# Seven block products for eight over half of the k tiles, in pairs of column tiles, with every loop written out

## The chip, the cores and the metric

The kernel runs on 1 core of one Trainium2 chip. The metric is the device time of one launch in microseconds: the median of the runs, 3132.33 us before (three runs, 3132.25 to 3133.17). TensorE multiplies, VectorE (DVE) and ScalarE (ACT) work on tiles, GpSimd (POOL) and SyncE (SP) here mostly issue DMAs.

## The reference

One layer of a hybrid decoder for a prompt of 512 rows and 8 single sampled rows with caches, all fp32. Cut to what matters:

```python
u = rms_norm(h, g_pre)                                   # (rows, 2048)
z = jnp.einsum('bsd,de->bse', u, w_in)                   # 176 column tiles of 128 are used
qa, ka, va, za, qr, kr, vr, zr, ga, gb = jnp.split(z, split_points, axis=-1)
# attention: 3 groups (window, dilation) x 8 heads, mixed by their softmax denominators
ya = combine_groups(outs, lses).reshape(B, S, A_WIDTH) * jax.nn.silu(za)
# retention: 8 heads, keys and values of 256, decay per head, root mean square norm per head
yr = (yr * rsqrt(mean(yr * yr) + EPS) * g_ret) * jax.nn.silu(zr)
merged = sigmoid(ga) * (ya @ w_a_out) + sigmoid(gb) * (yr @ w_r_out)
h = h + rms_norm(merged @ w_o, g_post)
h = h + sigmoid(h @ w_ple_gate) * (p @ w_ple_proj)
```

The outputs are also the new windows of keys and values (for the sampled rows a copy of the caches moved by one row) and the new retention states.

## The kernel before

All activations stand transposed: `U` ("moving") holds 16 k tiles of 128 features by 520 columns (512 prompt rows and 8 sampled ones, `TC` = 520, `HC` = 260). Precision comes from two parts: every operand is split into a rounded part (hi) and the rest (lo), and a product is three passes, hi x hi, hi x lo, lo x hi.

The work is cut into units. A unit is one column tile of a weight matrix (128 columns): `unit` (L462) runs 16 k tiles x 3 passes x 2 halves of 260 columns = 96 matmuls into two PSUM banks of `acc`, which has two such accumulators used in turn. There are 176 units over `u` (10 for each of 8 attention heads, 8 for each of 8 retention heads, 4 in each of 8 rounds of gates), then 16 each for `w_a` (8 k tiles), `w_r`, `w_o` and `w_gate`. The mean times of the trace carry the line of the matmul, L475.

The weights of a unit come by one DMA of 1 MB on SyncE's queue (`load`, L402) into one of two slots of `raw`, and behind it a piece of the cache copies from DRAM to DRAM (`keep_rows`, L365). ScalarE rounds all 2048 elements in one instruction (`hi`, L818, L821), VectorE subtracts (`lo`, L1136, L1139) and raises `s_wready`; TensorE waits for that and for `s_accfree`. ScalarE also takes a finished unit out of PSUM (`head_tile` L893, `residue_tile` L899, gates L1028).

Between k tiles of a unit hang hooks: the small matmuls and transposes of the head's own work, at places written out by hand (`attention_head` L612, `retention_head` L721). Each waits for its inputs: `exchange` (L568) for `spread_stats` on VectorE, `prob_turn` (L578) for the probabilities, `head_rows` and `ret_rows` for a finished tile, `ret_scores` and `ret_values` for PSUM banks and decayed scores, `sample_states` (L711) for the new states of half of the sampled rows, `sample_values` for weighted value rows. VectorE does in program order, unit by unit: row copies, `masked_far`, `masked_near`, `maxima`, `spread_stats`, `shares`, `normed`, `sample_keys` (L1307), `sample_columns` (L1405), `sample_states` (L1425), `scaled_keys`, `decayed`, and `ret_output` (reciprocal, scaling, gate; L1517 to L1525), with `lo` after the rest of the unit.

The heads after the first (for retention after the second), the gate rounds after the second and the projections run as hardware loops on every engine, with wait values worked out in registers (`Tally`, `Waits`).

## Time and profile before

| | before |
|---|---|
| median of the runs | 3132.33 us |
| the profiled execution | 3126.95 us |
| its span, first to last instruction | 3125.4 us |
| TensorE busy | 3026.9 us, 97% |
| VectorE busy | 1128.4 us, 36% |
| ScalarE busy | 827.4 us, 26% |
| mean granted TensorE clock | 0.987 |
| matmuls of 260 columns in L475 | 22,080 |

The busy time of TensorE is that of a pipelined stream, so the cost of one matmul is read from the start and end of a long run of them, and not from the mean duration of one. "Issue" as the reason of an idle stretch is time in which the engine waited for nothing that the profile shows. Idle time of an engine off the path costs nothing. The stages are: to 60 us the transposes, the norm and the projection of `p`; to some 1120 us the attention heads; to some 2040 us the retention heads; to 2410 us the gates; then the four projections.

### The profile page before, as it was taken

What the parts mean: (1) busy time and instruction counts of PE and PEld (TensorE: products, weight loads), DVE (VectorE), ACT (ScalarE), POOL (GpSimd) and SP (SyncE); (2) the same over time, 40 slices, a digit from 0 to 9 for tenths busy, and PEclk for the clock granted to TensorE, in tenths of its full rate; (3) what the DMA queues carried; (4) which work ended last, traced back from release to release, by engine and by line L of the source; (5) the groups of instructions that cost most, each with busy time, mean ns of one, the idle gap of its engine ahead of it and who ended that gap; (6) DMA issues with size and microseconds to landing.
All of it is one profiled execution on the core that took longest, in us unless ns stands there. A gap on an engine that the chain in (4) does not pass through costs nothing.

```text
span 3125.4 us, 58547 instructions
## 1 busy us (share of the span) xinstructions
PE 3026.9 (97%) x24438; PEld 2975.1 (95%) x24438; DVE 1128.4 (36%) x1325; ACT 827.4 (26%) x1065; POOL 369.7 (12%) x553
## 2 busy tenths in 40 slices
PE   7999999999999999999999999999999999999798
PEld 7999999999999998999999999999999999999798
DVE  5324233242323323453443443352222343322632
ACT  6223232222322222222222222222122221222222
POOL 2000000000000000220221121121000100100410
PEclk9999999999999999999999999999999999999899
DMA  9665646565565644654654554577655576755352
GB/s 312 201 202 188 209 155 210 187 200 195 167 217 182 198 136 127 192 163 126 189 177 125 181 169 139 179 238 248 212 193 171 170 253 201 248 166 169 108 179 77
DMA packets 534990, 574.97 MB, mean 184 GB/s; under 512 B 15560, under 2 KB 495624, under 8 KB 531592
## 3 DMA queue, kind: packets, MB, share of 16 engines
q1 hardware_dynamic: 490944, 428.31, 43.2%
q0 software_dynamic: 43856, 143.69, 14.0%
q8 instruction: 173, 2.83, 0.4%
q14 instruction: 17, 0.14, 0.0%
HBM read 515.67 MB, written 232.42 MB: 239 GB/s over the span
## 4 chain that ended last, share of the span: by engine, by line
PE 94%; DVE 2%; issue 1%; ACT 1%; DMA 1%; DVEq 0%; ACTq 0%; SPq 0%; POOL 0%; POOLq 0%
PE acc L475 84%; PE aux L648 1%; PE aux L658 1%; PE aux L667 1%; PE aux L717 1%; DVE stage_buffers L1670 1%; PE aux L547 1%; PE aux L603 0%; PE aux L554 0%; PE aux L641 0%; PE aux L675 0%; PE aux L708 0%; PE acc L538 0%; PE aux L574 0%; PE aux L588 0%
## 5 line engine op out<-in xcount | busy, mean ns | idle before, releaser
L475 PE MATMUL acc<-moving,weights 128*128 128x260 f32 x22080 | 2748.1, 285 | 45.2 <-issue 32.7
L475 PEld LDWEIGHTS acc<-moving,weights 128*128 128x128 f32 x22080 | 2687.6, 189 | 61.7 <-issue 49.3
L1139 DVE TENSOR_TENSOR weights<-raw_weights,weights 128x2048 fp32r<-128x2048 f32 (+1 forms) x242 | 538.8, 2226 | 1299.4 <-ACT weights L821 1284.0
L821 ACT ACTIVATE weights<-raw_weights 128x2048 fp32r<-128x2048 f32 (+1 forms) x242 | 451.3, 1865 | 213.4 <-PE acc L475 204.4
L896 ACT ACTIVATE stage_buffers<-acc 128x520 f32<-128x520 f32 x96 | 58.1, 605 | 854.6 <-PE acc L475 854.4
L902 ACT ACTIVATE stage_buffers<-acc 128x260 f32<-128x260 f32 x48 | 30.9, 643 | 394.8 <-PE acc L475 394.8
L1707 POOL DMA_DIRECT2D out<-stage_buffers x72 | 50.0, 694 | 670.1 <-DVEq L1222 507.0
L1028 ACT ACTIVATE stage_buffers<-acc 128x520 f32<-128x520 f32 x32 | 19.4, 606 | 264.6 <-PE acc L475 257.0
L1788 POOL DMA_DIRECT2D out<-stage_buffers x64 | 45.5, 715 | 135.0 <-DVEq L1447 123.5
L1740 POOL DMA_DIRECT2D stage_buffers<-in_cache_win x24 | 21.7, 905 | 333.4 <-DVE sample_keep L1312 230.0
L1431 DVE SCALAR_TENSOR_TENSOR stage_buffers<-stage_buffers,sampled 128x256 f32<-128x256 f32 x128 | 52.1, 479 | 13.7 <-ACT stage_buffers L975 13.6
L1707 POOL DMA_DIRECT2D sg_scr<-stage_buffers x32 | 17.4, 543 | 306.3 <-ACTq L1029 281.0
L1684 DVE TENSOR_TENSOR stage_buffers<-stage_buffers 128x520 f32<-128x520 f32 x16 | 11.2, 701 | 116.6 <-ACTq L1116 116.6
L1879 POOL TENSOR_TENSOR stage_buffers<-stage_buffers 128x520 f32<-128x520 f32 x16 | 27.0, 1696 | 218.7 <-DVE stage_buffers L1670 218.7
L1630 DVE TENSOR_TENSOR stage_buffers<-acc,stage_buffers 128x520 f32<-128x520 f32 x16 | 11.2, 698 | 112.1 <-PE acc L475 112.1
L1655 DVE TENSOR_TENSOR stage_buffers<-stage_buffers 128x520 f32<-128x520 f32 x16 | 11.2, 701 | 110.6 <-ACTq L1093 110.6
L489 PE MATMUL acc<-moving,weights 128*128 128x260 f32 x192 | 28.5, 306 | 18.3 <-DVE moving L1674 18.3
L1777 POOL DMA_DIRECT2D stage_buffers<-in_state_ret x64 | 45.3, 713 | 6.9 <-issue 4.3
L489 PEld LDWEIGHTS acc<-moving,weights 128*128 128x128 f32 x192 | 26.1, 207 | 20.9 <-issue 13.0
L1707 POOL DMA_DIRECT2D vrow_scr<-stage_buffers x8 | 4.1, 513 | 348.7 <-DVEq L1507 348.7
L1781 POOL DMA_DIRECT2D stage_buffers<-vrow_scr x64 | 45.0, 709 | 0.0
L1707 POOL DMA_DIRECT2D y_scr<-stage_buffers x24 | 13.2, 549 | 267.3 <-DVE stage_buffers L1525 125.6
(230 smaller groups left out, 1626.0 us busy)
## 6 DMA issues: line engine op xcount, KB each, us to landing
raw_weights<-in_w_in SPq DMA_DIRECT2D x176, 1024.0 KB, 5.8
out<-in_cache_win SPq DMA_DIRECT2D x128, 1023.5 KB, 8.5
out<-in_cache_win SPq DMA_DIRECT2D x32, 1022.0 KB, 7.9
out<-stage_buffers POOLq DMA_DIRECT2D x120, 256.0 KB, 3.3
stage_buffers<-in_cache_win POOLq DMA_DIRECT2D x48, 512.0 KB, 7.1
stage_buffers<-in_state_ret POOLq DMA_DIRECT2D x64, 256.0 KB, 5.6
raw_weights<-in_w_r_out SPq DMA_DIRECT2D x16, 1024.0 KB, 6.0
raw_weights<-in_w_o SPq DMA_DIRECT2D x16, 1024.0 KB, 5.8
```

The costliest lines, as they stand in the source:

```text
L475: mm = pe.matmul(acc[:, par, half, 0:HC], W[:, par, wp, k, :], U[:, up, k, a:b], start=(k == ks[0] and n == 0), stop=(k == ks[-1] and n == 2))
L489: mm = pe.matmul(acc[:, par, half, 0:HC], W[:, par, wp, k, :], U[:, up, k, a:b], start=(k == 0 and n == 0), stop=(k == KD - 1 and n == 2))
L547: mm = pe.transpose(aux[:, bank, tb * P:(tb + 1) * P], src[:, tb * P:(tb + 1) * P], ident[:])
L648: mm = pe.matmul(aux[:, bank, 0:T - jb * P], rk[:, j, jb * P:(jb + 1) * P], rq[:, j, jb * P:T], start=(j == 0), stop=(j == 1))
L821: act.activation(W[:, par, 0, 0:k], raw[:, par, 0:k], ACT.Copy).then_inc(s_whi, 1)
L896: act.activation(halves(dst), acc[:, par, :, 0:HC], func, scale=scale).then_inc(ready, 1)
L1139: dve.tensor_tensor(W[:, par, 1, 0:k], raw[:, par, 0:k], W[:, par, 0, 0:k].bitcast(F32), ALU.subtract).then_inc(s_wready, 1)
L1431: dve.scalar_tensor_tensor(out=r_st[:, half, b, j, :], in0=r_v[:, half, b, :], scalar=zs[:, bass.ds(h * 2 * NS + at, 1)], in1=r_st[:, half ...
L1707: pool.dma_start(dst, src).then_inc(stored, 16)
L1777: pool.dma_start(r_st[:, half, b], state[0, half * HB + b, bass.ds(h, 1)].rearrange("o (j p) e -> p (o j) e", p=P)).then_inc(s_rst[half], 16)
L1781: pool.dma_start(r_v[:, half, b].rearrange("p (e c) -> p e c", e=2), v_src[b:b + 1].broadcast_to([P, 2, P])).then_inc(s_rst[half], 16)
L1788: pool.dma_start(ret_s[0, half * HB + b, bass.ds(h, 1)].rearrange("o (j p) e -> p (o j) e", p=P), r_st[:, half, b]).then_inc(s_rnewst[half ...
```

## The change

**The product.** Of the 88 pairs of units over `u`, 86 are computed by Strassen's scheme in Winograd's form over the last eight k tiles. The two column tiles of a pair, the two groups of 4 k tiles (8 to 11, 12 to 15) and the two halves of the columns make 2 x 2 x 2 blocks. Seven block products of 4 k tiles x 3 passes = 12 matmuls stand in for eight. Four combinations of the moving blocks are made once, in the first pairs (`combine_blocks`, into `V` and into `U[:, :, 8:12, HC:TC]`). Four sums of weight blocks are made for every pair on VectorE, inside `lo`. The first eight k tiles stay as they were. The products add up partly in PSUM and partly by way of `part`: ScalarE copies three half banks of a pair out (`s_read`), VectorE one (`s_read7`), and VectorE makes the final tiles with additions (`evict`).

**The order.** A pair is 11 operations (steps) of 12 or 24 matmuls. `W` becomes a ring of 6 chunks of 4 k tiles (`AHEAD`): `hi` and `lo` work on 512 elements for the operation six ahead. `raw` holds one pair in two halves of eight k tiles (before: two slots), each loaded when its last reader of the pair before is done. The heads' small work hangs on the 11 steps on all engines. Row copies go from VectorE to ScalarE; taking out finished u tiles goes from ScalarE to VectorE; SiLU and sigmoid become their own operations on ScalarE.

**The rest.** All loops are written out, and wait values are constants. Sampled states go two rows at a time (`QB`), not four; the third group of value rows is loaded into the second's buffer. `pp_out` has 8 tiles, not 16. `X` has 8 tiles and the residual sum is made in `M`. The projections are plain pairs in chunks of 4 k tiles. The number of cache copies is the same; in attention and gates two are issued behind each pair's loads.

```diff
+OPS = {"S": [("sum", 0), ("raw", 3, 0), ("raw", 0, 0), ("raw", 1, 0), ("raw", 2, 0), ("raw", 2, 1), ("raw", 3, 0),
+             ("sum", 0), ("raw", 3, 1), ("raw", 0, 1), ("raw", 1, 1)],
...
+AHEAD = 6
...
-    W = stack.enter_context(nc.sbuf_tensor("weights", [P, 2, 2, KD, P], F32R))
-    raw = stack.enter_context(nc.sbuf_tensor("raw_weights", [P, 2, KD, P], F32))
+    W = stack.enter_context(nc.sbuf_tensor("weights", [P, AHEAD, 2, 4, P], F32R))
+    raw = stack.enter_context(nc.sbuf_tensor("raw_weights", [P, 2, 8, 2, P], F32))
...
+        def load(p, half):
+
+            sp.wait_ge(s_wready, read_until[p.nth, half] + 1)
...
+        for p in pairs:
+            for half in halves_of(p):
+                load(p, half)
+            q = p.nth
+            if q < RET:
+                for j in range(2):
+                    keep_rows(sp, 2, q // 5, 2 * (q % 5) + j)
...
+        def strassen_pair(p, hooks):
+            g = p.first
+            for n in range(p.n):
+                for f in hooks.get(n, ()):
                     f()
+                pe.wait_ge(s_wready, g + n + 1)
+                if n == 0:
+                    acc_ready(0)
+                    mm = product(g + n, 0, 1, moving(8, 1), True, True)
+                elif n == 1:
+                    mm = product(g + n, 0, 0, moving(12, 0), True, False)
+                elif n in (2, 3):
+                    product(g + n, 0, 0, moving(4 * (n - 2), 0), False, n == 3)
+                    if n == 2:
+                        pe.wait_ge(s_read, 3 * p.sums + 1)
+                    mm = product(g + n, 0, 1, moving(4 * (n - 2), 1), False, False)
+                elif n == 4:
+                    acc_ready(1)
+                    mm = product(g + n, 1, 1, moving(8, 0), True, True)
+                elif n == 5:
+                    mm = product(g + n, 1, 0, combined(1), True, True)
+                elif n == 6:
+                    mm = product(g + n, 0, 1, moving(12, 1), False, True)
+                elif n == 7:
+                    pe.wait_ge(s_read, 3 * p.sums + 2)
+                    mm = product(g + n, 1, 1, combined(0), False, True)
+                elif n == 8:
+                    pe.wait_ge(s_read7, p.sums + 1)
+                    mm = product(g + n, 1, 0, combined(2), False, False)
+                else:
+                    product(g + n, 1, 0, moving(4 * (n - 9), 0), False, n == 10)
+                    if n == 9:
+                        pe.wait_ge(s_read, 3 * p.sums + 3)
+                    mm = product(g + n, 1, 1, moving(4 * (n - 9), 1), False, n == 10)
+                mm.then_inc(s_used, 1)
...
+        for h in range(H):
+            hooks = [
+                {2: [row_turn], 4: [values]} if h else {},
+                {},
+                {2: [lambda: head_rows(kT[:, 0, :], 2)], 4: [lambda: head_rows(kT[:, 1, :], 0)],
+                 5: [lambda: scores_far(1)], 6: [lambda: scores_near(0)], 8: [lambda: scores_near(1)]},
+                {2: [lambda: head_rows(kT[:, 2, :], 1)], 3: [lambda: scores_far(2)], 10: [exchange]},
+                {2: [lambda: head_rows(vT[:, 0, :], 0)], 4: [lambda: head_rows(vT[:, 1, :], 0)],
+                 6: [lambda: prob_turn(0)], 7: [lambda: prob_turn(1)], 8: [lambda: prob_turn(2)],
+                 9: [lambda: prob_turn(3)], 10: [lambda: head_rows(vT[:, 0, :], 0)]},
+            ]
...
+        STATE_AT = {(0, 8): [lambda: sample_states(0)], (1, 2): [lambda: sample_states(1)],
+                    (1, 7): [lambda: sample_states(0)], (2, 1): [lambda: sample_states(1)]}
...
+                {2: [lambda: ret_rows(rk, 0, 2, 0)], 3: [lambda: ret_rows(rk, 1, 0, 1)], 5: [lambda: ret_scores(0)],
+                 6: [lambda: ret_scores(1)], 8: [lambda: ret_scores(2)], 9: [lambda: ret_scores(3)]},
+                {1: [sample_values] if h >= 2 else [], 2: [lambda: ret_rows(rv, 0, 0, 0)],
+                 3: [lambda: ret_rows(rv, 1, 0, 1)], 5: [vrow_turn], 6: [lambda: ret_values(0)],
+                 7: [lambda: ret_values(1)], 8: [ret_state], 10: [ret_norm]},
...
+        def lo(g):
...
+            if strassen and n == 0:
+                dve.wait_ge(s_wload[1], 16 * loads_due[p.nth, 1])
+                dve.drain()
+                dve.tensor_tensor(tmp_w[:], raw_chunk(2, 1), raw_chunk(3, 1), ALU.add).then_inc(s_sum, 1)
...
+            if strassen and n == 1:
+                dve.drain()
+                dve.tensor_tensor(raw_chunk(2, 1), raw_chunk(2, 0), raw_chunk(2, 1), ALU.subtract)
+                dve.tensor_tensor(tmp_w[:], tmp_w[:], raw_chunk(2, 0), ALU.subtract)
+                dve.drain()
+                dve.tensor_tensor(raw_chunk(3, 0), raw_chunk(3, 0), tmp_w[:], ALU.subtract).then_inc(s_sum, 1)
...
+        def steps(p, tiles, hooks, scale=1.0):
+
+            g = p.first
+            for n in range(p.n):
+                if p.mode == "S":
+                    if n == 5:
+                        dve.wait_ge(s_read, 3 * p.sums + 2)
+                        evict(p, 0, 0, tiles[0], scale)
+                        dve.wait_ge(s_used, g + 6)
+                        dve.scalar_tensor_tensor(out=part[:, 0, :], in0=acc[:, 1, 0, 0:HC], scalar=scale, in1=part[:, 0, :],
+                                                 op0=ALU.mult, op1=ALU.add).then_inc(s_read7, 1)
+                    if n == 7:
+                        dve.wait_ge(s_read, 3 * p.sums + 3)
+                        evict(p, 0, 1, tiles[0], scale)
+                    if n == 10:
+                        dve.wait_ge(s_used, g + 11)
+                        for half in range(2):
+                            evict(p, 1, half, tiles[1], scale)
...
+                for f in hooks.get(n, ()):
+                    f()
+                lo(g + n + AHEAD)
...
+                { 4: [lambda: masked_far(2, h), lambda: maxima(1)],
+                 8: [lambda: sample_keys(2, h - 1)] if h else [], 9: [spread_stats]},
+                {0: [gaps], 2: [shares, normed],},
...
+            return {(0, 4): [lambda: sample_states(0, h)], (0, 9): [lambda: sample_states(1, h), lambda: sample_ret_y(0, h)],
+                    (1, 3): [lambda: sample_ret_y(1, h), lambda: sample_states(2, h)],
+                    (1, 8): [lambda: sample_states(3, h), lambda: sample_ret_y(2, h)],
+                    (2, 2): [lambda: sample_ret_y(3, h)]}
...
+            return {(1, 5): [lambda: sample_columns(i)], (2, 10): [lambda: last_sample_columns(i)],
+                    (3, 3): [lambda: sample_output(i)]}
```

In the tables of hooks a key (j, n) is pair j of a head and step n; on TensorE a hook runs before operation n, on VectorE after the evictions of step n and before its `lo`. `ret_output` hangs on (0, 1), `scaled_keys` on (2, 4), `decayed` on (2, 6), (2, 7), (2, 9) and (2, 10).

## Rows read from the trace of the kernel before

**Rows 1.** The page, busy time, share of the span and instructions.
```profile
PE 3026.9 (97%) x24438; PEld 2975.1 (95%) x24438; DVE 1128.4 (36%) x1325; ACT 827.4 (26%) x1065; POOL 369.7 (12%) x553
```

**Rows 2.** Windows by stage: busy (instructions) by engine, PEclk, DMA share, GB/s.
```profile
100.00:1250.00 1150.00, 1124.08 (x9150) 1113.42 (x9149) 379.27 (x429) 304.94 (x501) 81.88 (x123) 0.99 0.57 184
1250.00:2100.00 850.00, 840.12 (x6581) 806.62 (x6581) 367.21 (x525) 214.47 (x237) 165.14 (x247) 1.00 0.55 169
```

**Rows 3.** Groups by line: busy us, mean ns of one | idle before.
```profile
L1139 DVE TENSOR_TENSOR weights<-raw_weights,weights 128x2048 fp32r<-128x2048 f32 (+1 forms) x242 | 538.8, 2226 | 1299.4 <-ACT weights L821 1284.0 <-DMA stage_buffers<-in_c_move 14.9
...
L875 ACT ACTIVATE moving<-stage_buffers 128x520 fp32r<-128x520 f32 x16 | 10.2, 636 | 5.5 <-PE acc L538 2.2 <-DVE stage_buffers L1201 1.8 <-issue 0.4
```

**Rows 4.** The waits: who waited for whom, us in total, times, longest.
```profile
DVE weights L1139 <- ACT weights L821: 1284.0, 221, 12.7
```

**Rows 5.** Timeline of TensorE: start, us, instructions in a row.
```profile
999.74 46.37 PE L475 MATMUL acc<-moving,weights 128*128 128x260 f32 x384
```

**Rows 6.** Timeline of the weight loads in `values`, one PSUM bank.
```profile
1119.41 1.87 PEld L603 LDWEIGHTS aux<-stage_buffers 128*128 128x128 f32 x16
```

**Rows 7.** Timeline at a turn of the attention loop, then two of the retention loop.
```profile
317.97 0.86 PE L475 MATMUL acc<-moving,weights 128*128 128x260 f32 x5 [1.50 <-issue]
320.77 6.92 PE L475 MATMUL acc<-moving,weights 128*128 128x260 f32 x43 [1.94 <-issue]
...
1463.05 28.88 PEld L475 LDWEIGHTS acc<-moving,weights 128*128 128x128 f32 x240 [1.99 <-issue]
...
1577.88 22.26 PEld L475 LDWEIGHTS acc<-moving,weights 128*128 128x128 f32 x185 [1.77 <-issue]
```

**Rows 8.** Windows behind a turn, and behind an idle of 2.7 us.
```profile
322.00:326.00 4.00, 4.00 (x23) 4.00 (x23) 0.00 (x0) 0.00 (x0) 0.56 (x1) 0.58 0.80 235
326.00:330.00 4.00, 4.00 (x36) 4.00 (x35) 0.29 (x1) 0.00 (x0) 0.00 (x0) 1.00 0.88 353
...
1243.00:1247.00 4.00, 4.00 (x23) 4.00 (x23) 0.00 (x0) 0.00 (x0) 1.22 (x3) 0.57 0.19 70
```

**Rows 9.** Timeline of VectorE in the norm, operations back to back.
```profile
45.05 0.75 DVE L1201 SCALAR_TENSOR_TENSOR stage_buffers<-stage_buffers,small 128x520 f32<-128x520 f32 x1
45.72 0.69 DVE L1208 TENSOR_TENSOR moving<-stage_buffers,moving 128x520 fp32r<-128x520 f32 x1
46.33 0.75 DVE L1201 SCALAR_TENSOR_TENSOR stage_buffers<-stage_buffers,small 128x520 f32<-128x520 f32 x1
```

**Rows 10.** Groups by line: the operations of VectorE's hooks.
```profile
L1310 DVE TENSOR_TENSOR stage_buffers<-stage_buffers 128x1024 f32<-128x1024 f32 x24 | 29.2, 1218 | 0.0
...
L1485 DVE TENSOR_SCALAR stage_buffers<-aux,small 128x128 f32<-128x128 f32 x64 | 18.0, 344 | 4.7 <-PE aux L641 2.2 <-issue 2.2
...
L1228 DVE SCALAR_TENSOR_TENSOR stage_buffers<-stage_buffers,small,aux 128x512 f32<-128x512 f32 x16 | 11.2, 744 | 2.5 <-issue 2.4
...
L1248 DVE TENSOR_REDUCE stage_buffers<-stage_buffers 128x4 f32<-128x1024 f32 x8 | 9.8, 1220 | 0.8
```

**Rows 11.** Timeline of VectorE in a retention head: `ret_output`, `sample_states`.
```profile
1466.01 3.34 DVE L1517 RECIPROCAL stage_buffers<-stage_buffers 128x512 f32<-128x512 f32 x1
...
1471.13 1.29 DVE L1525 TENSOR_TENSOR stage_buffers<-stage_buffers 128x512 f32<-128x512 f32 x2
...
1493.84 3.26 DVE L1431 SCALAR_TENSOR_TENSOR stage_buffers<-stage_buffers,sampled 128x256 f32<-128x256 f32 x8 [2.64 <-ACT stage_buffers L975]
...
1498.58 1.67 DVE L1444 SCALAR_TENSOR_TENSOR stage_buffers<-stage_buffers,sampled 128x256 f32<-128x256 f32 x4 [0.17 <-issue]
```

**Rows 12.** DMA issues: size, median us from issue to landing.
```profile
raw_weights<-in_w_in SPq DMA_DIRECT2D x176, 1024.0 KB, 5.8
out<-in_cache_win SPq DMA_DIRECT2D x128, 1023.5 KB, 8.5
...
pp_scr<-stage_buffers POOLq DMA_DIRECT2D x4, 1040.0 KB, 10.8
```

**Rows 13.** Timeline of the weight loads before the second gate projection unit.
```profile
2939.01 4.46 PEld L475 LDWEIGHTS acc<-moving,weights 128*128 128x128 f32 x24 [4.56 <-DVE weights L1139]
```

1826 lines of the change are left out of this document (949 added, 877 removed).

## The prediction

> **What bounds the kernel now.** I read the page's engine shares first: TensorE is busy 97% of the span, 3026.9 of 3125.4 us [rows 1]. The stage table then says that this holds in the attention stage (100 to 1250 us) and in the retention stage (1250 to 2100 us), with VectorE busy 33% and 43% there [rows 2]. The costly groups show why VectorE is busy at all: half of it is L1139 (`lo`), one subtraction of 2048 elements per unit, 2.23 us each [rows 3], after the copy of L821 (`hi`) on ScalarE. The waits show that it has slack: VectorE waited 1284 us for `hi`, which itself waits for a whole unit of 96 matmuls [rows 4]. So TensorE's stream sets the end. In it 384 matmuls of 260 columns run in 46.37 us, 0.1203 us each once the last one's own latency is off [rows 5]. That is the price of a matmul.
>
> **Matmuls removed.** Of the 88 pairs of u units, 86 take the new scheme (the first two stay plain). Such a pair had 192 matmuls; now it has 96 over the first eight k tiles and 7 x 12 over the last eight, 180. 86 x 12 x 0.1203 = -124.1 us. Twelve in a row now write one PSUM bank where before two banks alternated. The nearest row is the 16 matmul halves of L603, which accumulate in one bank at 0.112 us for 128 columns of plain fp32 [rows 6]; that is two passes of the columns and no more, so I take no price for it. Bounds: 0 and 0.012 us on each of the 7224, +87.
>
> **Loops removed.** At each turn of the attention loop TensorE stood idle 1.50 and 1.94 us for "issue" [rows 7], and for 4 us behind it the granted clock was near its lower level, 1.2 GHz: 23 matmuls in 4 us and not 36 [rows 8]. That is 5.0 us a turn, seven turns, -35. The retention loop shows one gap of 1.99 or 1.77 us between weight loads at each of five turns [rows 7], some 1.6 of it lost, -8; the clock stays. At the seams between stages, of which the wait of 4.56 us for weights at 2939 is one [rows 13], the finer weight chunks make the next weights ready early. I count 17 us of such idle that goes and 6 that comes (the last tile before the gate projection is followed by more matmuls, and the last two output turns stand at the end): -11.
>
> **The start.** `pp_out` shrinks to 8 tiles, so ScalarE waits from the ninth for a store that takes 10.8 us to land [rows 12]: +8. In the first plain pair VectorE now stops at op 2 for the last such store and combines the moving blocks (8 operations of 1040 elements, about 1.15 us each, twice the rate of [rows 9]), and three more at op 6, before it evicts at op 7. TensorE is done with that pair 23.1 us after its start and needs the accumulator; by my count VectorE gives it 9 us later. +10 (0 to +15).
>
> **What each pair now costs VectorE.** Operations of 520 elements start 0.61 to 0.67 us apart, waits included, and end 0.69 us after their start [rows 9]. A pair has 11 `lo` of 512 (6.9 us), four weight sums with drains (3.0 us), and the evictions that ScalarE did (5 operations of 252 or 260 elements, two small, drains: 2.8 us): 12.7 us where two `lo` took 4.5. TensorE needs 21.65 us for a pair. [...]
>
> The average therefore fits; the order is what hurts. Each engine runs its list in order, and TensorE now waits for VectorE inside the pair: at op 8 for `s_read7` (VectorE's step 5), at op 9 and at op 2 for partial sums, at op 0 for the accumulator, and at every hook. Count from the end of op k, e_k: without hooks e0 1.4, e2 5.8, e4 10.1, e7 14.4, e8 15.9, e9 18.8, e10 21.7 us (12 matmuls 1.44 us, 24 matmuls 2.89). Weights for op k+6 are ready 1.5 us after e_k (a copy of 520 on ScalarE takes 0.64 [rows 3], the subtraction 0.69, and handovers). The next pair's half buffer can be asked for after `lo` of op 8, at e2+1.5, and a load of 1 MB lands 5.8 us later [rows 12]: 13.5 us. From there VectorE does sum, `lo`, `lo`, three sums, eviction, three `lo` and reaches step 10 at 21.7, just as TensorE does; part 0 is copied by 23.6 and wanted at 26.0. A pair without hooks costs no stall, with 2.4 us to spare.
>
> **Attention, fourth pair of a head.** e3 is 9.9 with its hooks. VectorE after it: `lo` 11.4; `masked_far`, `maxima` (0.74 and 1.22 [rows 10], drains) 13.7; `lo` 14.3; eviction and seventh product 15.2; sum, the trip to ScalarE and back 17.3; `lo` 17.9; sums 20.2; eviction 21.0; `lo` 21.6; `sample_keys` (two of 1.22 us [rows 10]) 24.1; `lo` 24.7; `spread_stats` 25.2. `exchange` stands before op 10 and waits for it, and TensorE is there at 20.1: 5.1 us. In the fifth pair `shares` and `normed` delay the load by 1.5 us, and `head_rows` of v and a bank cost 1.3; the second pair 0.2. An idle of 2.7 us before 1243 us was followed by 23 matmuls in 4 us [rows 8], 1.5 us lost, so I add 1.7. Seven heads x 8.3 and 4 in the first: +62. What this part gives in matmuls and loops is inside the terms above.
>
> **Retention, a head from the third on.** First pair: ScalarE's `ret_gate` is done at 4.7, `lo` at 6.0; then `ret_output`, 6.3 us of reciprocal, scaling and gating [rows 11], to 12.2; three `lo` 14.0; `sample_states` for two samples, half of the 6.4 us that [rows 11] show for four plus its drains, 3.6 us, to 17.6; `lo`, eviction, seventh product: 19.1. TensorE is at op 8 at 14.4 and has 0.95 us of its own hook there: 3.75 us. With `sample_states` again at step 9, twice in the second pair, and 3.9 us of `sample_columns` (three operations of 1024 elements [rows 10]) VectorE has 57 us of chain in two pairs where TensorE has 46: stalls of 0.8 (part 0), 1.4 (part 2 at op 9, ScalarE held by the late sum), 1.65 (`sample_states` hook of the third pair). In the third pair `scaled_keys` (8 of 0.344 [rows 10]) holds the scores 1.3 and `decayed` 1.4; the last columns at step 10 hold `sample_values` 3.0, the v rows 0.3. Together 13.6 us; six heads 82, second head 11, first 2. The clock behind the stalls of 3 us: +10 to +14, I take 14. Sum +109.
>
> **Gates.** The last head's work falls into pairs 0 to 7 without TensorE's hooks to cover it: 3.75+0.8+1.4+1.65+2.5+2.5, clock 2: +14.
>
> **The sum.** 3125.4-124.1-35-8-11+8+10+62+109+14 = 3150 us of span. The profiled run took 3126.95 us for its span of 3125.4, and the median of the runs is 3132.33, so the median lies 6.9 us over the span: 3157 us. No part of the sum is larger than the stalls, 185 us of it. Under 0.2% (6.3 us) a measurement of this kernel can't tell a change from none.
>
> **Rivals.** (a) *The stalls swallow one another.* A wait at op 8 gives VectorE and the load time that the next one then doesn't need; I followed that through in the retention head, but only within it. Against it: `exchange` and op 8 stand behind pure VectorE work. For it: the average, 12.7 of 21.65 us before hooks. If 40% of the 185 remain: 3157-111 = 3046, with 55% 3074, with 30% 3027. (b) *No stall at all*, the change as written: 3157-185-10 = 2962. The waits speak for slack [rows 4], the in-order lists against it. (c) *The load is late, the slower side.* One pair's raw weights now sit in a single buffer and two cache copies of 8.5 us each [rows 12] are queued at once behind the load of half 0. If half 1 lands after 8.2 us and more, the 2.4 us of slack are gone, and each of the 86 pairs pays what lies over it; with the queue's 8.5 us and the hooks that already use the slack, about 0.7 us a pair: +60, 3217. It decides from a landing of 8.2 us. (d) *The matmuls don't get cheaper*, because one bank at a time costs 0.012 us each: +87, 3244.
>
> **Chances.** The sum as worked out 0.50, from 3110 to 3200 by itself (0.10 of it under 3126, 0.08 within 0.2%); (a) 0.28, nearly all faster; (b) 0.05; (c) 0.14; (d) 0.03. Faster 0.05+0.27+0.10 = 0.42, same 0.08, slower 0.50. The range leaves out (b) and the high ends of (c) and (d): 3027 to 3225 us.
>
> **What the changed profile would show.** Right: 21,048 matmuls of 260 columns; no "issue" gaps of 2 us; VectorE near 57% (1128 us before, plus 8.2 us for each of 86 pairs, less 33 us of row copies that go to ScalarE); TensorE idle of 5 us before `exchange` in each head from the second on, and of 3 to 4 us before op 8 in each retention head's first pair; a retention head of some 123 us where a turn of the loop took 114.8 (1463.05 to 1577.88 [rows 7]); gates faster than before. Wrong: if idle of TensorE in the two stages stays under 60 us, (a) or (b) holds; if VectorE's first sum waits for the load in most pairs, (c); if a run of 12 matmuls takes over 1.5 us, (d). The weakest step is the order inside the retention head, then the 0.62 us for each small operation, which enters it some fifteen times a pair.

## The result, and the profile after

The changed kernel takes 3308.03 us (median of four runs, 3301.25 to 3311.07) against 3132.48 of the kernel before in the same session: a ratio of 1.0557, 95% interval 1.0539 to 1.0575. Slower was forecast, by 0.8%; it is 5.6%, and 3308 lies outside the range of 3027 to 3225. The profiled run has a span of 3308.8 us.

The page of the changed kernel, engine shares and granted clock, to be read beside [rows 1]:

```profile
PE 3017.6 (91%) x23406; PEld 2950.6 (89%) x23406; DVE 1760.2 (53%) x3159; ACT 1122.3 (34%) x2078; POOL 361.8 (11%) x537
...
PEclk8999999999999899899999999999999999999799
```

TensorE has 1032 matmuls less and is busy for only 9 us less. That is the first hint: matmuls worth 124 us are gone, and 115 us came back inside the busy time. The stages tell where. Their limits are found by counting matmuls of 260 columns (in both kernels: start of the u units, start of retention, of the gates, of the projections). Columns: length, busy time and instructions of TensorE, of its weight loads, VectorE, ScalarE, GpSimd; granted clock, DMA share, GB/s. First before, then after:

```profile
60.20:1122.10 1061.90, 1038.60 (x8512) 1033.18 (x8513) 347.97 (x394) 287.88 (x479) 72.25 (x108) 0.99 0.60 194
1122.10:2036.80 914.70, 903.86 (x7034) 865.45 (x7033) 372.78 (x516) 225.59 (x258) 158.13 (x236) 1.00 0.52 159
2036.80:2415.60 378.80, 377.08 (x3143) 376.80 (x3142) 106.95 (x102) 89.39 (x73) 40.77 (x68) 1.00 0.66 217
2415.60:3125.40 709.80, 665.82 (x5463) 660.31 (x5462) 264.69 (x253) 182.82 (x196) 82.36 (x112) 0.98 0.54 173
```

```profile
71.20:1182.10 1110.90, 1022.36 (x8034) 1013.56 (x8035) 625.64 (x1138) 397.99 (x808) 72.20 (x108) 0.94 0.55 183
1182.10:2210.80 1028.70, 919.22 (x6674) 870.94 (x6673) 596.99 (x1142) 330.86 (x574) 159.78 (x238) 0.94 0.42 141
2210.80:2589.60 378.80, 363.85 (x2950) 361.97 (x2950) 221.12 (x396) 150.03 (x274) 29.51 (x43) 0.97 0.61 219
2589.60:3308.80 719.20, 668.23 (x5462) 662.85 (x5460) 279.15 (x408) 200.19 (x347) 84.08 (x120) 0.97 0.51 175
```

Idle is length less busy. The column "clock" is what is left of the change in busy time once the removed matmuls (0.1203 us each) are taken off. In us against before, measured, and what the prediction had put there:

| | matmuls | idle | clock | sum | predicted idle, clock, sum |
|---|---|---|---|---|---|
| start | | | | +11 | +8 |
| attention (first pair in it) | -55 | +65 | +39 | +49 | +36, +1, -18 |
| retention | -46 | +99 | +62 | +114 | +87, +14, +55 |
| gates | -23 | +13 | +10 | 0 | +12, +2, -9 |
| projections, seams | | | | +9 | -11 |
| all | -124 | +177 | +110 | +183 | +25 |

That the column is time at the lower clock can be read directly: busy time times what the granted clock lacks to 1, added up over windows of 1 us, is 135 us in the changed kernel and 26 in the one before, 109 more (attention 43, retention 51, gates 10; some 4 us of the 62 are hooks of the last attention head that now stand behind the border). So the idle was 42 us above the prediction's 135, and the clock 93 above its 17.

Timeline of TensorE in an attention head of the changed kernel: start, length, instructions, and in brackets the idle time before them with what ended it:

```profile
314.65 3.58 PE L690 MATMUL aux<-stage_buffers 128*128 128x8 f32 x16 [5.08 <-DVEq L1496]
...
352.36 0.43 PE L730 MATMUL aux<-ident,small 128*72 128x128 f32 x1 [2.29 <-ACTq L1061]
...
395.70 8.96 PE L532 MATMUL acc<-moving,weights 128*128 128x260 f32 x60 [2.38 <-ACT partial_sums L1010]
```

L690 is `exchange`: 5.08 us, where 5.1 was worked out. L730 (`row_turn`) and the partial sum in the head's second pair were not in the sum. The stretches behind the first of them (columns as above):

```profile
308.00:312.00 4.00, 1.57 (x14) 1.36 (x12) 3.75 (x7) 1.67 (x3) 0.00 (x0) 1.00 1.43 569
312.00:316.00 4.00, 1.35 (x7) 1.35 (x7) 3.19 (x6) 0.00 (x0) 0.00 (x0) 0.82 0.00 0
316.00:320.00 4.00, 4.00 (x20) 4.00 (x21) 0.00 (x0) 0.00 (x0) 0.00 (x0) 0.50 0.00 0
320.00:324.00 4.00, 4.00 (x30) 4.00 (x30) 1.13 (x4) 0.63 (x1) 0.00 (x0) 0.83 0.01 4
```

After 5 us without work the clock is at its lower level (0.50, 1.2 GHz) until some 321 us, and a stretch of 4 us holds 20 instructions and not 36. And a retention head, the same view:

```profile
1658.58 2.84 PE L833 MATMUL aux<-one,stage_buffers 128*128 128x1 f32 x16 [2.73 <-DVEq L1651]
...
1674.95 0.28 PE L803 MATMUL aux<-ident,small 128*16 128x128 f32 x1 [1.68 <-ACT stage_buffers L1109]
...
1713.24 1.18 PE L843 MATMUL aux<-one,stage_buffers 128*128 128x1 f32 x8 [2.69 <-DVEq L1679]
1714.79 2.94 PE L532 MATMUL acc<-combined_moving,weights 128*128 128x260 f32 x12 [0.37 <-DVE partial_sums L1409]
...
1752.38 1.02 PE L843 MATMUL aux<-one,stage_buffers 128*128 128x1 f32 x8 [1.52 <-DVE sample_keep L1683]
```

12 us of idle in 127 (13.6 were worked out), but in pieces: `sample_values` 2.73, `vrow_turn` 1.68, `sample_states` 2.69 and 1.52. The 12 matmuls of L532 that start at 1714.79 take 2.94 us and not the 1.6 of a quiet stretch. Here each piece of near 3 us has its stretch at 1.2 GHz behind it, as the row behind 2.73 shows (same columns):

```profile
1660.00:1664.00 4.00, 4.00 (x19) 4.00 (x20) 0.00 (x0) 0.00 (x0) 0.00 (x0) 0.50 0.00 0
```

That the scheme itself does what it says is seen in the gates, where few hooks hang. VectorE's first weight sum of each pair there:

```profile
2470.70 0.69 DVE L1290 TENSOR_TENSOR combined_weights<-raw_weights 128x512 f32<-128x512 f32 x1
...
2492.26 0.69 DVE L1290 TENSOR_TENSOR combined_weights<-raw_weights 128x512 f32<-128x512 f32 x1
```

A pair in 21.56 us (21.65 worked out), where two units took 23.1.

### The profile page after: what moved, and what is told of

It is laid out like the page before. It is cut to its first block, busy times and chain, and to the rows that moved or that the text cites. A ratio compares the mean times of both kernels' runs of the same rounds, so it can differ in the third digit from the quotient of the medians.

```text
span 3308.8 us, 56669 instructions
## 1 busy us (share of the span) xinstructions
PE 3017.6 (91%) x23406; PEld 2950.6 (89%) x23406; DVE 1760.2 (53%) x3159; ACT 1122.3 (34%) x2078; POOL 361.8 (11%) x537
## 3 DMA queue, kind: packets, MB, share of 16 engines
q0 software_dynamic: 43600, 143.69, 13.5%
## 4 chain that ended last, share of the span: by engine, by line
PE 65%; DVE 12%; DMA 11%; DVEq 4%; ACT 4%; issue 2%; ACTq 1%; SPq 1%; POOL 0%; POOLq 0%
PE acc L532 38%; PE acc L544 18%; DMA raw_weights<-in_w_in 7%; DVE weights L1293 3%; ACT weights L941 2%; PE aux L777 1%; DVE stage_buffers L1668 1%; PE aux L766 1%; DVEq L1716 1%; PE aux L787 1%; PE aux L690 1%; DVE stage_buffers L1883 1%; DVE stage_buffers L1635 1%; PE aux L833 1%; DMA stage_buffers<-vrow_scr 1%
## 5 line engine op out<-in xcount | busy, mean ns | idle before, releaser
L532 PE MATMUL acc<-moving,weights 128*128 128x260 f32 x12384 | 1634.4, 292 | 42.5 <-ACT partial_sums L1010 42.5
L532 PEld LDWEIGHTS acc<-moving,weights 128*128 128x128 f32 x12384 | 1580.4, 197 | 53.2 <-ACT partial_sums L1010 46.6
L1293 DVE TENSOR_TENSOR weights<-raw_weights,weights 128x512 fp32r<-128x512 f32 (+1 forms) x1030 | 692.1, 685 | 1039.3 <-ACT weights L941 993.9
L941 ACT ACTIVATE weights<-raw_weights 128x512 fp32r<-128x512 f32 (+1 forms) x1030 | 625.6, 623 | 1376.5 <-PE acc L532 733.0
L544 PE MATMUL acc<-moving,weights 128*128 128x260 f32 x5760 | 708.8, 285 | 48.1 <-DVE moving L1853 19.6
L544 PEld LDWEIGHTS acc<-moving,weights 128*128 128x128 f32 x5760 | 702.3, 191 | 52.4 <-DVE weights L1293 26.2
L532 PE MATMUL acc<-combined_moving,weights 128*128 128x260 f32 x3096 | 426.2, 290 | 2.1 <-DVE partial_sums L1409 2.1
L532 PEld LDWEIGHTS acc<-combined_moving,weights 128*128 128x128 f32 x3096 | 395.4, 192 | 7.7 <-issue 6.4
L941 ACT ACTIVATE weights<-combined_weights 128x512 fp32r<-128x512 f32 x172 | 108.0, 628 | 396.2 <-DVE combined_weights L1290 321.1
L1374 DVE SCALAR_TENSOR_TENSOR stage_buffers<-acc,partial_sums 128x260 f32<-128x260 f32 x344 | 154.3, 477 | 125.9 <-PE acc L532 121.9
L1010 ACT ACTIVATE partial_sums<-acc 128x260 f32<-128x260 f32 x258 | 98.8, 383 | 253.3 <-PE acc L532 177.2
L1293 DVE TENSOR_TENSOR weights<-combined_weights,weights 128x512 fp32r<-128x512 f32 x172 | 118.7, 690 | 115.8 <-ACT weights L941 115.4
L690 PEld LDWEIGHTS aux<-stage_buffers 128*128 128x128 f32 x128 | 26.3, 313 | 37.0 <-DVEq L1496 37.0
L690 PE MATMUL aux<-stage_buffers 128*128 128x8 f32 x128 | 27.0, 349 | 35.4 <-DVEq L1496 35.4
```

Source lines behind the costliest of these rows:

```text
L532: mm = pe.matmul(acc[:, m, half, 0:HC], W[:, g % AHEAD, wp, kk, :], mov(up, kk), start=(start and kk == 0 and n == 0), stop=(stop and kk = ...
L544: mm = pe.matmul(acc[:, m, half, 0:HC], W[:, g % AHEAD, wp, kk, :], moving(first, half)(up, kk), start=(start and kk == 0 and n == 0), sto ...
L690: mm = pe.matmul(aux[:, 1, way * 2 * TB:(way + 1) * 2 * TB], move[:, way, n, :], spread[:, way, n].rearrange("p q c -> p (q c)"), start=(n ...
L941: act.activation(W[:, g % AHEAD, 0, 0:src.shape[1]], src, ACT.Copy).then_inc(s_whi, 1)
L1010: act.activation(part[:, i, :], acc[:, m, half, 0:HC], ACT.Copy, scale=scale_of(p)).then_inc(s_read, 1)
L1293: dve.tensor_tensor(W[:, g % AHEAD, 1, 0:src.shape[1]], src, W[:, g % AHEAD, 0, 0:src.shape[1]].bitcast(F32), ALU.subtract).then_inc(s_wre ...
```

## The experiments

### Eight products in the new frame

```diff
-add_pair("S", w_in, (base + h * RK, base + h * RK + P))
+add_pair("F1", w_in, (base + h * RK, base + h * RK + P))    # and so for all 86 pairs
+hooks of step n stand at step 8 * n // 11 on every engine
```

> All 86 pairs with eight products again (8 steps of 24 matmuls on two banks, hooks of step n of 11 at step 8n/11), everything else of the changed kernel kept: written-out loops, six chunks of weights, raw pair buffer, small lo and hi, evictions on VectorE. Theory A (the seven-product scheme's weight sums and partial sums make TensorE wait, and the clock behind the waits adds to it): the waits for partial_sums and for the exchange go, 124 us of matmuls come back; 3132 - 43 (loops) + 20 (start) = about 3110, between 3090 and 3140. Theory B (not the scheme but the new order of the hooks, the small weight chunks and the single pair buffer make the waits): the waits stay and 124 us come on top, about 3430.

3293.22 us (ratio 1.0524). Neither theory holds. The waits behind partial sums are gone, but the retention head still waits, now 4.16 us for `sample_values`, and the coarse steps bring waits of their own (2.43 for a tile, since both tiles of a pair now end together, and 1.32 for the accumulators). From three heads:

```profile
347.24 0.66 PE L666 MATMUL aux<-ident,stage_buffers 128*128 128x128 f32 x4 [2.43 <-DVEq L1405]
...
1575.96 3.10 PE L550 MATMUL acc<-moving,weights 128*128 128x260 f32 x24 [1.32 <-DVE sampled L1380]
...
1635.07 3.03 PE L840 MATMUL aux<-one,stage_buffers 128*128 128x1 f32 x16 [4.16 <-DVEq L1658]
```

What follows: a loss of this size comes about without the scheme's partial sums, from the frame around it (where the hooks stand, small chunks). It does not share the changed kernel's loss out: 69 us of this run's idle are waits at places where the changed kernel has none (for tiles 20.7 and 19.5, for the accumulators 15.2, before `values` 13.9), which the coarse steps brought. Its lower clock costs 58 us, not 135: behind the wait of 2.43 us the granted clock stays at 1.00 in seven of eight heads.

### Is the lower clock caused by the idle?

```diff
 def exchange(g=None):
+    pe.wait_ge(s_wready, g + 1)
+    for _ in range(30):
+        pe.matmul(acc[:, 1, 1, HC:512], W[:, g % AHEAD, 0, 0, :], U[:, 0, 4, 0:252], start=True, stop=True, ...)
     pe.wait_ge(s_stats, count.due(s_stats))
```

> 30 additional matmuls of 252 columns into an unused part of a bank ahead of the exchange in heads 1 to 7, results unused; they fit (3.5 us) into the 4.5 to 5.1 us that TensorE waits there. Theory D (idle time of TensorE is what lowers its clock afterwards, 10.2 us at the lower level behind most of these waits, so about 5 us lost each): the wait before exchange shrinks to 1.3 us, the clock stays at its upper level, 7 x 3.5 to 5 = 25 to 35 us less: about 3278. Rival (the clock falls for another reason, or the additional matmuls cost what they take): 3308 or more.

3282.77 us. The same with the products written to `aux[:, 1, 0:252]`, which `exchange` overwrites:

> As the kernel with 30 additional matmuls of 252 columns before the exchange in heads 1 to 7, but into the exchange's own bank, which the exchange overwrites, so that no sum is touched. Theory D (idle of TensorE is what lowers its clock): as there, wait before exchange 1 to 1.5 us, the 16 small matmuls of the exchange in 1.95 us and not 3.58, 3283 (3276 to 3290). Rival: 3300 or more.

3281.56 us (3277.2 to 3287.0), 26 us less with 210 matmuls more. Timeline of TensorE, then the stretches behind it, in this second kernel:

```profile
309.89 3.67 PE L690 MATMUL aux<-moving,weights 128*128 128x252 f32 x30
314.69 1.95 PE L694 MATMUL aux<-stage_buffers 128*128 128x8 f32 x16 [1.13 <-DVEq L1501]
316.50 6.00 PE L532 MATMUL acc<-moving,weights 128*128 128x260 f32 x48
```

```profile
312.00:316.00 4.00, 2.87 (x26) 2.66 (x24) 3.23 (x6) 0.00 (x0) 0.00 (x0) 1.00 0.13 53
316.00:320.00 4.00, 4.00 (x35) 4.00 (x35) 0.33 (x1) 0.34 (x1) 0.00 (x0) 1.00 0.00 0
```

`exchange` starts at the same time as before (314.69), takes 1.95 us and not 3.58, and the clock stays at 1.00. VectorE still ends this wait; only the idle is shorter. 26 us over seven heads is 3.7 us a head, paid for the clock alone; the prediction had 1.7. It is a low count: in four of the seven heads (waits of 1.1 to 2.6 us were left there) a stretch at the lower level still follows. So idle before it is a cause of the lower clock.

### The place of `spread_stats`

```diff
-8: [lambda: sample_keys(2, h - 1)] if h else [], 9: [spread_stats]},
+9: [spread_stats], 10: [lambda: sample_keys(2, h - 1)] if h else []},
```

> VectorE does spread_stats at step 9 before sample_keys(2), which goes to step 10. The changed kernel waits 4.5 to 5.1 us before exchange in seven heads. Theory A (VectorE's list in order is the cause): 2.5 us of each wait go, 7 x 2.5 = 17, and about half as much again or more in the clock behind it: 3308 - 17 - 15 = 3276. Rival (the wait only moves, to the partial sums of the same or the next pair): within 8 us of 3308.

3295.96 us, but the runs lie from 3276 to 3305. The wait before `exchange` goes from 5.1 to 2.65 us as expected; in the next pair `prob_turn` waits up to 2.65 us for ScalarE, which is held behind a late weight sum: `sample_keys` now stands ahead of what asks for its weights, and VectorE waits 4.49 us for them at 334.76 (1.40 in the changed kernel). `exchange` waits 15.7 us less in all, and 11.9 came back before `prob_turn`.

### Why the weights are late in a head's second pair

In the changed kernel, SyncE and GpSimd issuing DMAs, then VectorE:

```profile
246.18 0.90 POOL L1948 DMA_DIRECT2D stage_buffers<-in_cache_win  x1 [13.19 <-DVE sample_keep L1546]
247.07 0.56 POOL L1949 DMA_DIRECT2D stage_buffers<-row_scr  x1
```

```profile
246.51 6.53 SPq L480 DMA_DIRECT2D raw_weights<-in_w_in  x4
253.09 3.43 SPq L439 DMA_DIRECT2D out<-in_cache_win  x2
```

```profile
256.17 0.69 DVE L1290 TENSOR_TENSOR combined_weights<-raw_weights 128x512 f32<-128x512 f32 x1 [5.35 <-DMA raw_weights<-in_w_in]
```

The weights of half 1 are asked for at 246.5 and the last of them land after 9.1 us; VectorE waits 5.35. First without the 80 cache copies of this stage:

```diff
 if q < RET:
-    for j in range(2):
-        keep_rows(sp, 2, q // 5, 2 * (q % 5) + j)
+    pass
```

> The 80 cache copies (1 MB each) of the attention stage are left out; all else as in the changed kernel. Theory C (late loads of the second half behind copies make VectorE's first weight sum late in each head's second pair, and TensorE waits 2.4 to 5.4 us for the partial sum): those waits go, 23 us in seven heads, with 15 to 20 us of clock: about 3268. Rival (the load is late because of the window loads of the same time, or because it is asked for late): within 10 us of 3308.

3303.66 us, no difference, and the wait for the partial sum is still there (4.48 us in the head shown above):

```profile
398.85 10.22 PE L531 MATMUL acc<-moving,weights 128*128 128x260 f32 x60 [4.48 <-ACT partial_sums L1009]
```

The copies, suspected in the prediction's rival (c), are not it. Then the window load, which `sample_keys(0)` releases:

```diff
-{2: [lambda: sample_keys(0, h - 1)], 8: [lambda: sample_keys(1, h - 1)]} if h
+{6: [lambda: sample_keys(0, h - 1)], 8: [lambda: sample_keys(1, h - 1)]} if h
```

> One move in the changed kernel: VectorE's sample_keys(0) from (1,2) to (1,6). Its end is what releases the window load of group 1 (two transfers of 512 KB on another queue), at 246.2 us, 0.3 us ahead of the weight load of half 1 at 246.5, which lands after 9.1 us and not 4 to 5. Theory (collision of the two): VectorE's wait of 5 to 8 us for raw_weights in each head's second pair goes, and with it the 2.4 to 5.4 us of TensorE and the clock behind: 3308 - 7 x 5 = 3273. Rival (sample_keys itself, 2.5 us of VectorE, makes the sum late): VectorE's wait for the load stays above 2 us, the time within 10 us of 3308 or VectorE is late elsewhere.

3334.26 us, 26 slower. VectorE's waits for `raw_weights` in these pairs fell from 5 to 8 us to 0.3 to 0.7 (249.19: 0.55). The sum starts 5.8 us after its load was asked for (at 243.41) and not 9.7, so the load itself became faster, and the collision was the cause of the delay. But the window load of group 1 now starts at 254.06, and `sample_keys(1)` two steps later waits for it with everything that stands behind it on VectorE:

```profile
254.06 0.90 POOL L1948 DMA_DIRECT2D stage_buffers<-in_cache_win  x1 [23.25 <-DVE sample_keep L1546]
```

```profile
264.35 1.22 DVE L1543 TENSOR_TENSOR stage_buffers<-stage_buffers 128x1024 f32<-128x1024 f32 x1 [6.59 <-DMA stage_buffers<-row_scr]
```

```profile
269.54 6.94 PE L532 MATMUL acc<-moving,weights 128*128 128x260 f32 x36 [6.99 <-ACT partial_sums L1010]
```

TensorE's wait grew from 2.8 to 7.0 us. The theory of the load was right and the price expected was wrong: the next link of the same chain was not moved with it.

### Moving hooks, stage by stage

Nothing is left out in these; hooks stand at other steps. At the start of the u units:

```diff
-{2: [combine_blocks], 6: [lambda: [combine_lo(n) for n in range(3)]]},
+{7: [combine_blocks]},        # combine_lo at step 0 of the next pair
```

> combine_blocks moved behind the evictions of the first plain pair (step 7), its hi and lo to the end of that pair and step 0 of the next. Theory A (the prediction's: VectorE does the combination before it takes the first pair out of PSUM, and TensorE waits for the accumulator): the wait of 11.97 us goes, and 10.2 us at the lower clock behind it: 3308 - 11 - 5 = 3292. Rival (the plain pair is held up anyway, by lo of the next weights): 3305 or more.

3296.04 us: 12 less (16 expected).

```diff
-10: [exchange]},                                  # TensorE, pair 3
+{0: [exchange], ...                               # pair 4
-{2: [row_turn], 4: [values]}
+{3: [row_turn], 5: [values]}
-{0: [gaps], 2: [shares, normed],}
+{1: [gaps], 3: [shares, normed], 8: [lambda: sample_keys(2, h - 1)]}
+sample_keys(0) at (1, 6), sample_keys(1) at (2, 10)
```

> Attention hooks moved, nothing left out: exchange, gaps, gap_exps, shares and normed one to two steps later; row_turn and values one step later; sample_keys(0) from (1,2) to (1,6), (1) from (1,8) to (2,10), (2) from (3,8) to (4,8), so that its window loads are not asked for together with the next pair's weights. Theory A (each wait is a matter of the place of a hook, and VectorE has room): per head 5.0 (exchange), 2.3 (row_turn), about 4 (second pair's partial sum, late load) of idle and 6.8 of clock go, 7 x 18 = 126, of which I expect two thirds: 3308 - 85 = 3223. Rival (VectorE is too full, waits only move): 3280 or more. On the late load: if the window loads delay it, VectorE's wait for raw_weights in the second pair goes from 5 to 8 us to under 1.5 us; if it is asked for late, it stays.

3188.61 us, 119 less where 85 were expected. TensorE at `exchange` in two heads that follow each other:

```profile
667.62 1.95 PE L690 MATMUL aux<-stage_buffers 128*128 128x8 f32 x16 [0.18 <-DVEq L1496]
...
789.32 1.95 PE L690 MATMUL aux<-stage_buffers 128*128 128x8 f32 x16 [0.24 <-DVEq L1496]
```

A head in 121.7 us (123.2 in the mean of seven); it was 139 in the changed kernel (from 314.65 to 1148.12 over six heads) and 134 before. VectorE and ScalarE do the same work as before the move. With both `sample_keys` moved, the window load comes over 10 us behind the second pair's weight load, and VectorE waits at most 2.4 us for weights in this stage.

```diff
-{(0, 8): sample_states(0), (1, 2): (1), (1, 7): (0), (2, 1): (1)}      # TensorE
+{(0, 10): sample_states(0), (1, 4): (1), (2, 0): (0), (2, 5): (1)}
-ret_scores at (2, 5), (2, 6), (2, 8), (2, 9); sample_values at (3, 1); sample_softmax at (0, 3)
+ret_scores at (2, 6), (2, 7), (2, 9), (2, 10); sample_values at (3, 4); sample_softmax at (0, 7)
```

> Retention hooks moved, nothing left out: ret_scores and decayed one step later, TensorE's sample_states two to four steps behind VectorE's (before two to four, now five), sample_values three steps later, sample_columns to (1,9), vrow_turn two later, head 1's sampled softmax from step 3 to 7 (its bias load is queued behind two stores). Theory A (places of hooks): of 11.9 us of idle and 6.8 us of clock in each of six heads, and of 18.9 plus 8 us in head 1, two thirds go: 3308 - 93 = 3215. Rival (the prediction's 57 us of VectorE's chain against 46 us of TensorE in two pairs is a lack of throughput, not of place): 3270 or more.

3249.81 us, 58 less where 93 were expected. The waits of a head are hardly shorter (10 us, not 12): of the 63 us between the two profiled executions some 21 are idle and some 44 clock. One term was a single wait in head 1, 2.47 us after the move. VectorE at step 3 and TensorE behind it, in the changed kernel:

```profile
1324.08 0.55 DVE L1603 TENSOR_TENSOR stage_buffers<-aux,stage_buffers 64x387 f32<-64x387 f32 x1 [9.10 <-DMA stage_buffers<-in_c_bias]
```

```profile
1333.61 0.69 PE L823 MATMUL aux<-stage_buffers,one 64*128 64x64 f32 x2 [18.89 <-DVEq L1617]
```

The bias is a load that GpSimd issues behind two stores that it waits for. All three moves together:

> The moves of the three kernels before this one together. Theory A: the gains add, 15 + 85 + 93: 3115, a little under the kernel before (3130). Rival (the engines' lists are coupled and the gains don't add, or the lower clock comes back at what waits are left): over 3160.

3124.83 us (ratio 0.999, 0.9974 to 1.0007): the gains add, 12 + 119 + 58 = 189 against 183. The attention stage is done (clock 0.99). A retention head still has 10 us of idle, here with the stretch behind the wait of 3.23 us as the last row:

```profile
1674.29 1.67 PE L532 MATMUL acc<-combined_moving,weights 128*128 128x260 f32 x12 [0.80 <-DVE partial_sums L1409]
...
1679.83 1.70 PE L532 MATMUL acc<-moving,weights 128*128 128x260 f32 x12 [2.42 <-ACT partial_sums L1010]
...
1734.41 1.13 PE L766 MATMUL aux<-stage_buffers 128*128 128x256 f32 x4 [3.23 <-DVE stage_buffers L1701]
...
1758.50 2.40 PE L777 MATMUL aux<-stage_buffers 128*128 128x512 f32 x8 [2.61 <-DVE sample_keep L1657]
...
1734.00:1738.00 4.00, 3.59 (x26) 3.49 (x27) 2.21 (x4) 0.00 (x0) 0.00 (x0) 1.00 0.00 0
```

The clock stays at 1.00 here, behind a wait longer than the 2.73 us that had 0.50 behind it in the changed kernel. The length of one wait does not settle what follows it, and no run tells what else does.

### Place or volume in the retention stage

First the blocks of `sample_states` spread over the four pairs, at (0,8), (1,1), (1,6), (3,2):

> On top of all the moves together (3125 us): VectorE's sample_states of a retention head at (0,8), (1,1), (1,6), (3,2), so that each of the four pairs stays under TensorE's 21.6 us; sample_output at (3,4); combine_lo behind the second plain pair. Of the 10.4 us of idle that a retention head still had (0.8 and 2.4 behind a late sum, 1.3, 3.2 before ret_scores, 2.6 before ret_values), two thirds should go, with 2 us of clock each, and 4 us at the second plain pair. Theory A (places): 3125 - 6 x 9 - 10 = 3061. Rival (VectorE's lists are full in this stage): 3110 or more.

3131.16 us: nothing. The waits only moved, to 3.41 us behind the eviction of step 10, which the block at (0,8) makes late:

```profile
1558.57 1.68 PE L532 MATMUL acc<-combined_moving,weights 128*128 128x260 f32 x12 [0.80 <-DVE partial_sums L1411]
...
1565.11 7.07 PE L532 MATMUL acc<-moving,weights 128*128 128x260 f32 x36 [3.41 <-ACT partial_sums L1012]
```

Counting by pair is not fine enough. Within a pair TensorE needs three things of VectorE soon: the eviction and the seventh product at step 5, the eviction at 7, that at 10. Between 10 and the next pair's 5 only `lo` stands, with weights ready for several operations. So the blocks go there:

```diff
+sample_states on VectorE at (1, 1), (1, 3), (2, 2), (3, 3); last_sample_columns at (3, 2)
+ret_scores at (2, 6), (2, 7), (2, 10), (3, 0); decayed at (2, 7), (2, 8), (3, 0), (3, 1)
```

TensorE's and ScalarE's parts of `sample_states` move along, and as in the run before `combine_lo` stands behind the second plain pair.

> Instead of the spread before this one, VectorE's blocks of a retention head stand only in steps 1 to 4 of a pair, behind the eviction of step 10 and ahead of the seventh product's of step 5: sample_states at (1,1), (1,3), (2,2), (3,3), last columns at (3,2), scores 2 and 3 and decayed 2 and 3 later by one more. Theory A' (a block of 3.2 us costs nothing between step 10's eviction and step 5's, and costs its length anywhere else): a head of 119 to 122 us falls to about 111, 3125 - 6 x 8 - 8 = about 3070. Rival (the four pairs together are too full): waits of 3 us move once more, 3110 or more.

3106.98 us (ratio 0.9933, 0.9919 to 0.9946). And the volume: the kernel with all three moves, and VectorE's arithmetic of `sample_states` left out:

> As all the moves together, but VectorE's arithmetic in sample_states is left out (8 operations of 256 elements, 3.2 us, four times a head; the signals stay; sampled states and sampled retention outputs are not computed). If volume on VectorE is what is left: a head falls from 119 to 122 us to the 108 that its matmuls take, 3125 - 7 x 11 = 3045. If place is: what waits behind ret_output (0.8 and 2.4) and before ret_values (2.6) stays, a head takes 114 and more, 3090.

3075.62 us: 49 us less for some 102 us of VectorE's work (8 x 4 x 3.2), between the two expected times (3045 for volume, 3090 for place). Waits of 0.8, 2.4 and 2.6 us stay in each head as they were; that of 3.2 falls to 0.8. So place was left beside volume. In the kernel with the early steps a head had:

```profile
1541.04 1.68 PE L532 MATMUL acc<-combined_moving,weights 128*128 128x260 f32 x12 [0.80 <-DVE partial_sums L1411]
...
1546.66 15.97 PE L532 MATMUL acc<-moving,weights 128*128 128x260 f32 x120 [2.51 <-ACT partial_sums L1012]
...
1572.03 1.84 PE L845 MATMUL aux<-one,stage_buffers 128*128 128x1 f32 x8 [4.19 <-DVE sample_keep L1686]
```

```diff
 def ret_output(h):                                  # at step 0, was 1
     dve.wait_ge(s_rstd, count.due(s_rstd))
-    dve.wait_ge(s_z, count.due(s_z, skip=1))
     dve.reciprocal(rrs, rrs)
...
+def ret_gated(h):                                   # at step 1
+    dve.wait_ge(s_z, count.due(s_z, skip=1))
-(1, 8): [lambda: sample_states(1)]                  # TensorE
+(1, 10): [lambda: sample_states(1)]
-(1, 7): [lambda: sample_ret_y(0, h)]
+(1, 6): [lambda: sample_ret_y(0, h)]
```

> On top of the kernel with the blocks in steps 1 to 4 (3107 us, a retention head of 119.5 us with idle of 0.8, 2.3 and 4.2): ret_output's reciprocal and scaling at (0,0), where VectorE waits 3.4 us for ScalarE's ret_gate anyway, only the gating at (0,1); VectorE's sample_ret_y(0) at (1,6) and TensorE's second sample_states at (1,10), so that bank 3 is free. Theory A' (place): the 4.2 and most of the 3.1 go, with 2 to 3 us of clock in each head: 3107 - 6 x 9 = 3053. Rival (volume): the waits turn up at the next step, 3095 or more.

3029.83 us against 3127.17 of the kernel before: 0.9689, 0.9668 to 0.9711. Nothing is left out in it. It is 3.1% faster than the kernel before and 8% faster than the changed one, with the operations of the changed kernel on every engine. Its page, its retention stage, and a weight load of `ret_norm` in two heads that follow each other:

```profile
PE 2915.2 (96%) x23406; PEld 2856.1 (94%) x23406; DVE 1754.7 (58%) x3159; ACT 1123.0 (37%) x2078; POOL 362.9 (12%) x537
```

```profile
1180.00:2030.00 850.00, 828.54 (x6413) 791.04 (x6412) 580.48 (x1124) 322.42 (x560) 163.53 (x241) 0.99 0.52 174
```

```profile
1504.57 0.19 PEld L798 LDWEIGHTS aux<-stage_buffers,mean_rk 128*128 128x128 f32 x1 [0.24 <-issue]
...
1614.64 0.19 PEld L798 LDWEIGHTS aux<-stage_buffers,mean_rk 128*128 128x128 f32 x1 [0.24 <-issue]
```

A head in 110.1 us (129 in the changed kernel, 114.8 before [rows 7]), clock 0.99, VectorE busy 68% of this stage (58% of the span). This last step gave 77 us by the medians and 63 between the profiled executions; of the 63, 45 are idle and some 19 less time at the lower clock (52 to 33 us, added up as above).

## Why the prediction was wrong, point by point

**Matmuls removed, right.** 21,240 of 260 columns are left of 22,272, which is 1032 less (the prediction's 21,048 leaves out 192 that stood in a line of their own before). A pair takes 21.56 us, and two runs of 12 in one bank start 1.43 us apart in a quiet stretch (at 248.32 and 249.75 us): rival (d) is out.

**Loops removed, right as far as seen.** No gap of 2 us for "issue" is left, and after the moves an attention head takes 121.7 us, 123.2 in the mean: 134 less 7.2 for matmuls is 126.8, less the 5.0 of a turn 121.8.

**The start, right in kind.** +11 (8 predicted), and 11.97 us at the first plain pair (10), with clock behind it; moving the combination away gave 12.

**VectorE's cost for a pair, right.** It is busy 1760 us; 1128 + 86 x 8.2 - 33 = 1800 was worked out. In the working of a pair, 13.5 us for the landing should be 13.1 by its own terms (5.8 + 1.5 + 5.8); the 2.4 us to spare go with 13.1.

**Idle in the stages, right in retention, too low in attention.** 177 us against 135; in attention 65 against 36. `exchange` 5.1 worked out, 4.5 to 5.1 seen. A retention head 13.6 against 12, though not by the same places: 3.75 before op 8 turned up as 2.69 at `sample_states` and 0.37. Missing were `row_turn` (2.29 us, eight times), the late load in the second pair (2.4 to 5.4 us in six heads) and the bias load in head 1 (18.9 us; 11 for that head). The first two stand behind hooks whose queues I had not followed: ScalarE's `keep_columns`, and GpSimd's window load that VectorE's `sample_keys` releases. Idle makes up 42 us of the 158 that the change is above the sum.

**The clock, the step that failed.** I took one row of before, 2.7 us of idle with 1.5 us lost behind it [rows 8], and applied it once a head in attention (1.7) and as 14 us in all for six retention heads, 28 us with the gates and 17 after what the removed turns give back. Both the count and the price were too small. The kernel before has 8 stretches below full clock in the two stages, the changed one has 43. An attention head has mostly three: behind `exchange` 3.2 to 4.8 us are lost, behind `row_turn` 1.5 to 1.7, behind the late partial sum 1.7 to 2.7. A retention head from the third on has two that lose 3.2 to 3.4 us each, behind 2.73 and 2.69 us of idle, and in some heads a third. 110 us, not 17: 93 us of the 158. The Trainium skill (TensorE: Matmul & The Clock Gate, "A second HAM failure mode: psum-queue depth-cycling") tells of a kernel whose array idles briefly between groups and pays in clock for it; the retention rows above agree, with 12 us of idle in pieces under 3 us and a granted clock of 0.94. The term was there and mis-sized: the count of waits per head, times the price of each, was never multiplied out.

**Seams and projections.** -11 predicted, +9 seen, 20 us of the 158; of it one new wait of 8.0 us for ScalarE's evictions in the first pair of the last projection, where both units end together.

**The rivals.** (a), that stalls swallow one another, was wrong in the changed kernel: it left 30 to 55% of the stalls, and the idle alone came to 177 us. (b), 2962 without stalls, is what the last kernel comes nearer to, 68 us above it. (d)'s 0.012 us a matmul stands in no row, and no run shows it. (c) was half right: a load does land late, 9.1 us against a limit put at 8.2, but in one pair of an attention head's five, and not because of the copies (3304 without them) but of a window load on another queue.

## What to carry to other kernels

When work of a co-processor moves into the middle of the main engine's stream, count for each block of it which event of the main stream it stands ahead of, step by step and not by averages: the same operations took 3308 or 3030 us by their place alone. Price every wait of the matmul engine at its idle plus the time at the lower clock behind it, times the number of waits. In the changed kernel that about doubled the waits of 2.7 to 5 us; in the kernels with moved hooks waits of 2.4 to 3.2 us often cost their idle alone, so take both as bounds. And moving a step moves what it releases: look for the transfer that its end starts, what that collides with, and who waits for it two steps later.

## What the runs showed of the hardware

A few matmuls that nobody needs are cheaper than idling: 30 of them before each of seven waits made the kernel 26 us faster. In three of the seven heads the clock then stayed at its upper level; over the whole kernel the time lost at the lower one fell from 135 to 101 us.

The length of a wait alone does not set the clock behind it: 2.73 us had a granted clock of 0.50 behind it in the changed kernel, 3.23 us had 1.00 with the hooks moved, and 2.43 us had 1.00 in seven of eight heads with eight products.

Where those matmuls were written matters. In the first of the two kernels they began with `start` in columns 260 to 511 of the bank in whose columns 0 to 259 the sum of ops 4, 7 and 9 was waiting for op 10; the stored value rows of group 1, which come from that bank, came out changed by up to 0.70 of their size. Written to the exchange's own bank they changed nothing. This agrees with the Trainium skill (PSUM — Partial Sum Buffer, "The four PSUM rules"): a matmul that starts a sum clears the marks of the whole bank, and the next accumulating one overwrites.

The weight transfers of 512 KB with rows of 512 bytes landed 6.7 to 9.1 us after their issue in the second pair of a head, where 1 MB had been asked for on another queue 0.3 us before, and 3.9 to 7.5 us in the four pairs that follow.
